# The second layer's memory K/V projection, split into eight jobs and issued inside chunk attention

## The reference

```python
    mem_n = rms_norm(mem, mem_norm_g)
    for layer in range(DEPTH):
        ...
            x = x + chunk_attention(rms_norm(x, c_norm_g[i]), c_w_qkv[i], c_w_out[i],
                                    c_q_norm_g[i], c_k_norm_g[i], c_rel_bias[i])
        x = x + memory_cross_attention(rms_norm(x, xa_norm_g[layer]), mem_n, xa_w_q[layer],
                                       xa_w_kv[layer], xa_w_out[layer], ...)
        x = x + swiglu(rms_norm(x, f_norm_g[layer]), f_w_gate[layer], f_w_up[layer], f_w_down[layer])

def memory_cross_attention(h, mem_n, w_q, w_kv, w_out, q_g, k_g):
    q = rms_norm((h @ w_q).reshape(bsz, seq, XA_HEADS, XA_HEAD_DIM), q_g).astype(F32)
    kv = (mem_n @ w_kv).reshape(bsz, n_mem, 2, XA_HEADS, XA_HEAD_DIM)
    k = rms_norm(kv[:, :, 0], k_g).astype(F32)
    v = kv[:, :, 1].astype(F32)
```

## Time and profile before

| What | Value |
|---|---|
| Median of three runs | 1745.67 us |
| Lowest and highest of the three | 1743.47 and 1748.47 us |
| Span of the profiled execution | 1737.0 us |
| Median of the runs less that span | 8.67 us |
| PE busy | 1649.4 us, 95% of the span |
| DVE, ACT, POOL busy | 776.2, 622.6 and 228.3 us |
| Chain that ended last, by engine | PE 87%, DVE 7%, ACT 3%, issue 2% |

### The profile page before, as it was taken

One profiled execution on the slowest core, in us unless ns is written; L12 is line 12 of the kernel. 1 busy time (PEld: TensorE's weight loads), 2 busy tenths in 40 slices (PEclk: granted clock), 3 DMA queues, 4 the chain that ended last, 5 costly groups with the idle time before them and its releaser, 6 DMA issues.

```text
span 1737.0 us, 22605 instructions
## 1 busy us (share of the span) xinstructions
PE 1649.4 (95%) x9358; PEld 1345.0 (77%) x9358; DVE 776.2 (45%) x1011; ACT 622.6 (36%) x1006; POOL 228.3 (13%) x305
## 2 busy tenths in 40 slices
PE   5989989999999999999999997899999999999999
PEld 4778788777768788888888885478776878888887
DVE  4668345453534444442234437835343454444222
ACT  6543333353524322221114335634452432222110
POOL 3853134010000211110000000000000021111000
PEclk9999999999999999999999998999999999999999
DMA  6611012134112333332223221214311233333221
GB/s 208 124 49 50 25 52 75 49 130 137 49 49 73 97 97 97 97 97 97 97 97 98 97 97 37 86 49 145 122 49 49 73 97 97 97 97 97 97 97 73
DMA packets 146801, 151.85 MB, mean 87 GB/s; under 512 B 8864, under 2 KB 109344, under 8 KB 146592
## 3 DMA queue, kind: packets, MB, share of 16 engines
q1 hardware_dynamic: 146720, 150.69, 28.2%
HBM read 147.53 MB, written 3.15 MB: 87 GB/s over the span
## 4 chain that ended last, share of the span: by engine, by line
PE 87%; DVE 7%; ACT 3%; issue 2%; DMA 0%; SPq 0%; POOL 0%; DVEq 0%; ACTq 0%
PE ps L325 24%; PE ps L327 24%; PE ps L326 24%; PE ps L1640 2%; PE ps L1617 1%; PE ps L1996 1%; DVE sb L602 1%; PE ps L956 1%; DVE w_lo_ab L297 1%; DVE sb L2066 1%; ACT w_hi L293 1%; PE ps L1234 1%; PE ps L417 1%; ACT sb L2038 1%; PE ps L1245 1%
## 5 line engine op out<-in xcount | busy, mean ns | idle before, releaser
L325 PE MATMUL ps<-h_hi,w_hi 128*128 128x512 f32 x864 | 337.4, 390 | 4.2 <-DVE w_lo L1810 3.9
L326 PE MATMUL ps<-h_lo,w_hi 128*128 128x512 f32 x864 | 336.2, 389 | 0.0
L297 DVE TENSOR_TENSOR w_lo<-raw,w_hi 128x2048 fp32r<-128x2048 f32 x70 | 160.4, 2292 | 389.8 <-ACT w_hi L293 389.8
L293 ACT ACTIVATE w_hi<-raw 128x2048 fp32r<-128x2048 f32 x84 | 160.7, 1914 | 430.3 <-PE ps L327 429.7
L327 PE MATMUL ps<-h_hi,w_lo 128*128 128x512 f32 x704 | 273.9, 389 | 0.0
L325 PEld LDWEIGHTS ps<-h_hi,w_hi 128*128 128x128 f32 x864 | 162.2, 188 | 38.5 <-issue 5.2
L326 PEld LDWEIGHTS ps<-h_lo,w_hi 128*128 128x128 f32 x864 | 162.2, 188 | 33.3
L1810 DVE TENSOR_TENSOR w_lo<-raw,w_hi 128x2048 fp32r<-128x2048 f32 x44 | 138.1, 3138 | 53.5 <-ACT w_hi L1792 53.5
L327 PEld LDWEIGHTS ps<-h_hi,w_lo 128*128 128x128 f32 x704 | 132.1, 188 | 27.7
L1792 ACT ACTIVATE w_hi<-raw 128x2048 fp32r<-128x2048 f32 x44 | 84.3, 1916 | 160.9 <-PE ps L327 160.9
L325 PE MATMUL ps<-w_hi,a_hi 128*128 128x512 f32 x352 | 137.3, 390 | 1.7 <-DVE up L1808 1.7
(11 more groups left out here) (370 smaller groups left out, 2667.8 us busy)
## 6 DMA issues: line engine op xcount, KB each, us to landing
raw<-in_f_w_gate SPq DMA_DIRECT2D x44, 512.0 KB, 4.0
raw<-in_f_w_up SPq DMA_DIRECT2D x44, 512.0 KB, 5.2
raw<-in_f_w_down SPq DMA_DIRECT2D x44, 512.0 KB, 4.2
raw<-in_xa_w_kv SPq DMA_DIRECT2D x16, 1024.0 KB, 5.0
raw<-in_c_w_qkv SPq DMA_DIRECT2D x12, 1024.0 KB, 5.1
raw<-in_ab_w_in SPq DMA_DIRECT2D x10, 1024.0 KB, 5.8
raw<-in_xa_w_q SPq DMA_DIRECT2D x8, 1024.0 KB, 5.0
raw<-in_xa_w_out SPq DMA_DIRECT2D x8, 1024.0 KB, 5.0
```

The costliest lines, as they stand in the source:

```text
L293: a.activation(w_hi[:, n % 2, :], raw[n % 2], ACT.Copy).then_inc(sem("w_hi"), 1)
L297: v.tensor_tensor(w_lo(n)[:, n % 2, :], raw[n % 2], w_hi[:, n % 2, :].bitcast(F32), ALU.subtract).then_inc(sem("w_lo"), 1)
L325: pe.matmul(out, a[0], b[0], start=start, stop=False)
L326: pe.matmul(out, a[0], b[1], start=False, stop=False)
```

## The change

The K/V projection of layer 1 leaves its place behind the out-projection. It becomes eight jobs (four column blocks j of 512 by two row tiles i of 128), each of 24 matmuls of 512 columns. Jobs 0 and 1 stand between and behind the scores of pairs 0 and 1. Job m+2 stands in pair m, for m from 0 to 5, cut into four slices of six matmuls, one behind every second group of transposes. The first job writes bank 6 and the second bank 7, all others bank 6; so the transposes now take turns in two banks, not three. ACT copies each job's bank to SBUF as it is. The norms of K are then made from SBUF, while the out-projection runs. The memory's split goes to POOL, between its masks, and earlier. Pieces are loaded and split in the new order, K/V before out-projection. The addresses of several tiles move, so that nothing is overwritten too early.

```diff
+        def mem_split_pool(g):
+            g.wait_ge(sem("mem_kept"), after("mem_kept", 1))
+            g.wait_ge(sem("ca_turned"), 8)
+            g.wait_ge(sem("c_mask"), after("c_mask", 4))
+            link(g, g.tensor_copy(mem_T1[0], memT), "mem_hi")
+            g.tensor_tensor(mem_T1[1], memT, mem_T1[0].bitcast(F32), ALU.subtract).then_inc(sem("mem_lo"), 1)
...
+        KV1_BANK = [6, 7, 6, 6, 6, 6, 6, 6]
+        def kv1_pe(pe, j, i, kh, ks=range(4)):
+            n = MT * j + i
+            if kh == 0 and ks[0] == 0:
+                if n == 0:
+                    pe.wait_ge(sem("mem_lo"), 1)
+                if n >= 2:
+                    kv1_copied(pe, n - 1)
+            w = take_split(pe, f"kv1{j}_{kh}", 4)
+            for k in ks:
+                kk = 4 * kh + k
+                ins = product(pe, ps[:, KV1_BANK[n], :], of(mem_T1, kk, slice(i * P, (i + 1) * P)), of(w, k), kk == 0, kk == KT - 1)
...
         def ca_turn_p_pe(pe, m):
...
-                if g >= 3:
-                    pe.wait_ge(sem(COPY[(g - 3) % 8][0]), 4 * ((g - 3) // 8) + COPY[(g - 3) % 8][1])
+                if g >= 2:
+                    pe.wait_ge(sem(COPY[(g - 2) % 8][0]), 4 * ((g - 2) // 8) + COPY[(g - 2) % 8][1])
...
-                    ins = pe.transpose(ps[:, 4 + g % 3, i * P:(i + 1) * P], p_c(m, e, i)[:, s * P:(s + 1) * P], ident)
+                    ins = pe.transpose(ps[:, 4 + g % 2, i * P:(i + 1) * P], p_c(m, e, i)[:, s * P:(s + 1) * P], ident)
                 ins.then_inc(sem("c_tr"), 1)
+                if e == 1 and m < 6:
+                    kv1_pe(pe, *divmod(m + 2, MT), s // 2, range(2 * (s % 2), 2 * (s % 2) + 2))
...
             ca_scores_pe(pe, 0)
+            kv1_pe(pe, 0, 0, 0)
             ca_scores_pe(pe, 1)
+            kv1_pe(pe, 0, 1, 0)
+            for i in range(MT):
+                kv1_pe(pe, 0, i, 1)
...
         def ca_act(a):
+            pieces_hi(a, "kv11_0")
+            kv1_copy_act(a, 0)
+            kv1_copy_act(a, 1)
+            pieces_hi(a, "kv11_1")
             for m in range(CH // 2):
...
+                        if n == 5 and m % 2 == 1 and m < 6:
+                            pieces_hi(a, f"kv1{m // 2 + 1}_1", 1)
+                if m < 6:
+                    kv1_copy_act(a, m + 2)
                 a.wait_ge(sem("c_o"), m + 1)
...
+                if m % 2 == 1 and m < 6:
+                    pieces_hi(a, f"kv1{m // 2 + 1}_1", 2)
...
         def ca_dve(v):
             sums(0)
+            pieces_lo(v, "kv10_1")
             sums(1)
             rescale(0, 0)
             rescale(0, 1)
+            pieces_lo(v, "kv11_0")
             for m in range(CH // 2):
                 if m > 0:
                     out_lo(m - 1)
+                    if m % 2 == 0 and m < 7:
+                        pieces_lo(v, f"kv1{m // 2}_1", 2)
...
+                    if n == 3 and m == 0:
+                        pieces_lo(v, "kv11_1")
...
+                if m % 2 == 1 and m < 6:
+                    pieces_lo(v, f"kv1{m // 2 + 1}_1", 1)
...
         @block.scalar
+                    kv1_norms_act(a)
                     for half in range(2):
                         pieces_hi(a, "cao1_1", half)
-                        squares_act(a, "x1", x, sq_junk, ss2, "co_x", (half,))
-                pieces_hi(a, f"kv{l}0_1")
+                        squares_act(a, "x1", x, x1_junk, ss2, "co_x", (half,))
+                    pieces_hi(a, "cao1_1", 2)
...
                 norm_root_act(a, f"x{l}", TT)
...
-                    mem_split_act(a)
```

More of the change, by code:

```diff
@@ new lines, in kv1_norms_act @@
+        def kv1_norms_act(a):
+            a.wait_ge(sem("kv1_raw"), 4)
+            sqrt_table(a)
+            for n in range(8):
+                i, h = n // XH, n % XH
+                if n >= 4:
+                    a.wait_ge(sem("kv1_sq"), after("kv1_sq", n - 3))
+                a.activation(k1_junk[:, (n % 4) * 256:(n % 4 + 1) * 256], xk_rows[1][:, i, h * XD:(h + 1) * XD], ACT.Square,
+                             accum_out=kss[:, i, h:h + 1]).then_inc(sem("kv1_sq"), 1)
+            a.wait_ge(sem("kv1_sq"), after("kv1_sq", 8))
+            a.activation(kr, kss, ACT.Sqrt, bias=pcol("eps"), scale=1.0 / XD).then_inc(sem("kv1_rt"), 1)
@@ L1484, in kv_wait, with kv1_norms_dve, kv_act @@
+        def kv1_norms_dve(v):
+            v.wait_ge(sem("kv1_rt"), after("kv1_rt", 1))
+            link(v, v.reciprocal(kr, kr), "dve_step")
+            for i in range(MT):
+                for j in range(2):
+                    r = xk_rows[1][:, i, j * 512:(j + 1) * 512].rearrange("p (h n) -> p h n", h=2)
+                    v.tensor_tensor(r, r, bc(kr[:, i, 2 * j:2 * j + 2], 2, XD), ALU.mult).then_inc(sem("kv1_k"), 1)
         def kv_wait(eng, l, j, i):
             rows_wait(eng, f"kv{l}", f"kv{l}{j}", MT, j, i)
-        def kv_act(a, l):
-            t = f"kv{l}"
+        def kv_act(a):
+            l, t = 0, "kv0"
@@ L2157, in _ @@
                 ca_sp(sp, h)
-            load_pieces(sp, "cao0_0", "cao0_1")
-            for h in range(4, CH):
+            load_pieces(sp, "kv10_0", "kv11_1")
+            for h in range(4, 8):
                 ca_sp(sp, h)
-            load_pieces(sp, "cao1_0", f"dn1_{FT // 2 - 1}")
+            load_pieces(sp, "kv12_0", "kv12_1")
+            for h in range(8, 12):
+                ca_sp(sp, h)
+            load_pieces(sp, "kv13_0", "kv13_1")
+            for h in range(12, CH):
+                ca_sp(sp, h)
+            load_pieces(sp, "cao0_0", f"dn1_{FT // 2 - 1}")
             for i in range(TT):
```

137 lines of the change are left out of this document (81 added, 56 removed).

## The result

| | Before | After |
|---|---|---|
| Median, in the comparison of 20 runs each | 1745.4 us | 1747.39 us |
| Lowest and highest | 1742.59, 1748.47 | 1745.53, 1749.95 |
| Span of the profiled execution | 1737.0 | 1744.9 |

The ratio of after to before is 1.0014, with a 95% interval of 1.0008 to 1.002. The change makes the kernel slower, by 2.0 us in the medians and no more than 3.5 by the interval. That is inside the 0.3% of which I said that it can't be told from none; with 20 runs each it can, and it lies on the other side of zero from the forecast of 1.3 us less.

The account below looks back on a forecast made before the run. PE, busy 95% of the span, was taken as the bound. Chunk attention grows 42.0 us, 43.3 are saved: 1.3 less, span 1735.7, plus the median's 8.67 above it, 1744.4 us; range 1740.5 to 1750.9.

Parts of the forecast that it names:

- The saving: From out-projection to query projection: the moved projection's matmuls go, less a new wait before the query projection; 43.3 us saved.
- seam: Transposes of x to query projection: PE waits 2.5 us for DVE's first low part of x, behind xq10_1's.
- the sum for chunk attention: All growth of chunk attention: terms of 40.2 us, less 0.7 of correction, plus 2.5 for the clock; 42.0 us.
- Opening and pair 0: Start of chunk attention: early products, slices and two new waits make pair 1 start 8.5 us later; no clock fall.
- Pairs 1, 3, 5: Odd pairs of chunk attention: slices fill waits, 13.7 us a pair, growth 4.0 each before the correction.
- Pairs 2 and 4: Even pairs: two low parts meet on DVE, waits of 3.5 us, 17.2 a pair, growth 7.5 each before correction.
- Pair 6, with the clock: Pair without slices: pieces on DVE delay copies, 10.9 us in place of 6.76, plus 2.5 for a lower clock.
- Pair 7: Last pair of chunk attention, without slices: growth of 0.6 us before the correction.
- The correction of 0.7 us: Paper gave the old order 9.80 us a pair, the trace 9.68; 0.1 taken off each of seven later pairs.
- the clock's rival: Clock also falls in pairs 2 and 4 and before the query projection: 3.3 us each, 1754.3 us; chance 0.20.
- Smaller waits: Chunk attention's waits for low parts, 16.2 us in all, are half or less: 1736.3 us; chance 0.25.
- Room by weight loads: If only weight loads fill PE, 5.1 us are free in a pair, jobs nearly hide: 1718.9 us; chance 0.03.

Follow-up runs that it names:

- e4: Changed kernel with the high and low parts of the query projection's second piece moved behind those of the turned x: 1744.26 us.
- e10: Changed kernel with the last two slices of each job in pairs 0 to 5 joined, three slices in place of four: 1748.08 us.
- e7: Changed kernel with 12 idle transposes of the identity added in each of PE's two waits of pair 6: 1744.22 us.
- e1: Changed kernel with the second low part of a column block moved behind DVE's first copy in pairs 2, 4 and 6: 1744.57 us.
- e2: Changed kernel with the first low part moved ahead of DVE's reductions in pairs 1, 3 and 5: 1743.65 us.
- e9: Changed kernel with both low parts and the query projection's piece moved, and the out-projection's second piece split later, in pair 6: 1737.88 us.
- e5: Kernel before the change, with two banks in place of three for the transposes of the probabilities, nothing else: 1761.12 us.
- e3: Changed kernel with both low parts moved: the first ahead of the reductions, the second behind DVE's first copy: 1741.2 us.

## Why the prediction was wrong

**The saving was right to the tenth.** Out-projection and seam lost 44.60 - 1.34 = 43.26 us; the forecast said 43.3. The query projection follows 6.18 us after the transposes of x (6.1 said), with PE waiting 2.46 (2.5 said), and e4 shows that the named instructions make that wait.

**The failing step is the sum for chunk attention:** 42.0 us forecast, 45.10 measured. The waits in it are the right ones but for one in pair 6; the terms are too small. The 3.1 us are more than the forecast gain of 1.3, so the sign turned. By its terms, where the forecast has 0.1 less in each of seven pairs:

| Term | Forecast | Measured |
|---|---|---|
| Opening and pair 0 | +8.5 | +9.25 |
| Pairs 1, 3, 5 | 3 x 3.9 | 4.17, 4.22, 4.21 |
| Pairs 2 and 4 | 2 x 7.4 | 7.58, 8.06 |
| Pair 6, with the clock | +6.5 | +6.90 |
| Pair 7 | +0.5 | +0.74 |

Three causes can be named. Together they are 1.9 of the 3.1 us.

1. *The correction of 0.7 us.* The paper working of the old order was 0.1 us a pair too long, and I took this off the new order. The new order's pairs are 0.1 to 0.2 longer than the paper has them (13.84 against 13.7). Here the error of the working did not carry over to another order of instructions. Without the correction the forecast would have been 1745.1, still 0.6 less than before; it alone does not turn the sign.
2. *The opening, 0.75.* The twelve and 36 products and two blocks of scores took 0.47 us more than their starts promised (pair 0's transposes begin 25.9 us behind the 64 transposes, 25.4 forecast), and pair 0 took 16.38 for 16.1. The largest piece, 0.23, is at the twelve products: 2.95 us from the first to the scores (1058.10 to 1061.05), 2.72 by their starts. It lies at their ends: the first is 0.34 ahead of the second and the last 0.32 ahead of the scores, where 0.227 was reckoned. The rest is in smaller places. That slices between transposes cost it, e10 refutes; no run tests the products' borders to the scores, and why they cost 0.1 each stays open.
3. *The clock in pair 4.* Pairs 2 and 4 have the same instructions and the same first wait. Pair 2 took 17.25, pair 4 17.73, with 3.4 us at 0.50. It was the clock's rival at a small scale, 0.5 us, where I had priced a place with 3.3: the lower level fell partly on a time in which PE waited anyway (the second wait was 0.59 us there, and 1.36 in pair 2). This was no accident of one profile: all four kernels in which both waits stand as here (changed kernel, e4, e7, e10) have the lower level in pair 4, beginning 91.2 to 91.3 us behind the 64 transposes, and none in pair 2. e1 takes the second wait away and e2 the first, and neither has it in pair 4. Why pair 4 and not pair 2 stays open.

The other 1.2 us are 0.2 in each odd pair beyond the correction (half of it at the scores with their wait, 3.32 against 3.21), 0.3 in pair 6 and 0.1 to 0.2 elsewhere. So the forecast was too fine for its working: a gain of 1.3 us was the difference of 42.0 and 43.3, and a stage of eight pairs was not known to 3 us.

**Right, by rows:** odd and even pairs differ by 3.4 us, and 3.5 was forecast for the two waits (idle time of 1.57 and 1.36, for 1.7 and 1.8; idle time counts from a matmul's modelled end, and by the starts the delays are 1.8 and 1.6); PE stands twice in pairs 2, 4 and 6; the opening has no lower clock. POOL's split was ready 1.1 us before PE asked, and no PE wait names it. In pair 6 one releaser was wrong. I had PE idle for 2.7 and 2.2 us, released by DVE's low part and by its copy; the first wait was 2.31 us for ACT's copy, behind the high part of the out-projection's second piece (e9). The clock's price there, 2.5 forecast, is 2.66 by e7. And one of the prediction's own signs of being wrong came: the clock fell before pair 6, in pair 4.

**The rivals.** The clock in more places: true of pair 4, false of pair 2 and of the seam, and a seventh of the price. The seam is the weaker case: of the seven kernels with its wait of 2.46 us, three (e1, e7, e10) have 3.4 us at 0.50 that begin in the wait or 1.3 us behind it, in the stretch that the cuts call same code; the five without the wait have none there. The point between 1.15 and 2.75 us that should decide was not found: 1.57 us was followed by the lower level in pair 4 and not in pair 2, and in e5 it came in pairs whose longest wait is 0.69. Smaller waits: false for the stage as it stands, where even pairs are 3.4 us longer than odd ones for 3.5 reckoned, but they can be made smaller, and then the time is 1741.2 (e3). Room by weight loads: false. Pair 1 has 8.85 us of weight loads in 13.84, where the kernel before has 4.55 in 9.68, and still the pair grew by 4.17 for a job of 5.44. The Trainium skill's measure by weight loads (Perfetto Trace Analysis, Identifying the Most-Contended Engine, which names the share of peak FLOPs beside it) does not give the room of a stage with so many short transposes.

## What to carry to other kernels

Work that one engine does without a pause saves nothing by moving into another stage's waits, unless the waits are there: sum the waits of the stage first, and take off what the move itself makes (a bank that it takes, parts of weights that queue in front of copies). Then look at every new wait for the instruction that stands in front of its releaser and that nobody needs yet; here the parts of seven pieces and one bank were worth 14 us, seven times the change itself. And a wait moved behind a pair comes back in the next one (e9), so count the queue to the stage's end before moving.
